# Differential attention: transposes ahead of the next item's scores, both maps in turns; output-scale copies and two weight loads first; GDN sums by direction

## What is computed

```python
def diff_attend(q, k, v, lam):          # 4 heads, 2 maps per head, 64 numbers each
    s = jnp.einsum('bqhcd,bnhcd->bhcqn', q, k, preferred_element_type=F32) * DIFF_QK ** -0.5
    pr = jax.nn.softmax(s, axis=-1)
    w = (pr[:, :, 0] - lam * pr[:, :, 1]).astype(v.dtype)
    return jnp.einsum('bhqn,bnhd->bqhd', w, v)

    def step(s, inp):                   # gated DeltaNet, per direction, chunk and head
        v_new = uc - jnp.einsum('bhck,bhkv->bhcv', wc, s)
        s_next = s * gl[..., None, None] + jnp.einsum('bhck,bhcv->bhkv', kt, v_new)
        o = jnp.einsum('bhck,bhkv->bhcv', qd, s) + jnp.einsum('bhcj,bhjv->bhcv', qkc, v_new)
        return s_next, o

    y = jnp.einsum(...)                 # merged branches @ w_out, times the layer's gate, plus residual
    new_lat = post_norm(h_lat, gate_x * out_x, ln_g[l], ln_b[l])
```

## Time and profile before

| | us |
|---|---|
| median of 3 runs | 2978.74 (2974.03 to 2988.12) |
| the profiled execution | 2976.96 |
| its span, first to last instruction | 2975.1 |
| PE busy | 2801.1 (94%) |
| DVE busy | 1541.9 (52%) |
| ACT busy | 1012.8 (34%) |
| mean granted TensorE clock | 0.987 |

### The profile page before, as it was taken

How to read it: one execution, slowest core, us unless ns; L and a number is a source line. 1 busy time by engine, 2 the same in 40 slices (tenths; PEclk the granted TensorE clock), 3 DMA queues, 4 the chain that set the end, 5 groups by cost and what they waited for, 6 DMA issues and landing times.

```text
span 2975.1 us, 44200 instructions
## 1 busy us (share of the span) xinstructions
PE 2801.1 (94%) x18238; PEld 2197.7 (74%) x18238; DVE 1541.9 (52%) x2683; ACT 1012.8 (34%) x1640; POOL 637.3 (21%) x261
## 2 busy tenths in 40 slices
PE   7999999999999999999997999899899999999997
PEld 1487888887788778886785438777776787887675
DVE  5546666326634443337745644667534554353756
ACT  0345343312222333224431234544332234332533
POOL 0121000222123111321023312100132331232036
PEclk9999999999999999999998999999999999999999
DMA  7511000324232112211134561000234321221034
GB/s 251 172 55 35 18 14 23 112 70 141 84 121 66 40 50 101 68 50 38 41 103 138 190 201 58 19 23 13 78 112 116 127 99 47 93 95 57 22 113 163
DMA packets 100453, 254.21 MB, mean 85 GB/s; under 512 B 10306, under 2 KB 32964, under 8 KB 99872
## 3 DMA queue, kind: packets, MB, share of 16 engines
q1 hardware_dynamic: 94314, 231.07, 23.8%
q10 hardware_dynamic: 5942, 20.33, 1.9%
HBM read 217.27 MB, written 34.08 MB: 84 GB/s over the span
## 4 chain that ended last, share of the span: by engine, by line
PE 77%; DVE 12%; ACT 4%; DMA 3%; issue 3%; POOL 1%; SPq 1%; ACTq 0%; DVEq 0%
PE ps L818 17%; PE ps L819 16%; PE ps L820 16%; PE ps L987 4%; PE ps L826 4%; PE ps L836 4%; PE ps L1315 3%; PE ps L1252 2%; PE ps L946 2%; PE ps L901 1%; DVE t_gcv L1956 1%; PE ps L930 1%; PE ps L1342 1%; DVE t_amx L2486 1%; DMA t_raw<-in_w_ada 1%
## 5 line engine op out<-in xcount | busy, mean ns | idle before, releaser
L779 POOL TENSOR_TENSOR t_wlo<-t_raw,t_whi 128x1024 fp32r<-128x1024 f32 x248 | 615.6, 2485 | 2306.7 <-ACT t_whi L1436 2306.6
L818 PE MATMUL ps<-t_u_hi,t_whi 128*128 128x512 f32 (+1 forms) x2368 | 862.7, 364 | 10.5 <-issue 4.2
L819 PE MATMUL ps<-t_u_lo,t_whi 128*128 128x512 f32 (+1 forms) x2368 | 831.7, 351 | 0.0
L820 PE MATMUL ps<-t_u_hi,t_wlo 128*128 128x512 f32 (+1 forms) x2368 | 828.8, 350 | 0.0
L1436 ACT ACTIVATE t_whi<-t_raw 128x1024 fp32r<-128x1024 f32 x248 | 262.3, 1057 | 936.0 <-PE ps L820 730.0
L818 PEld LDWEIGHTS ps<-t_u_hi,t_whi 128*128 128x128 f32 x2368 | 448.3, 189 | 85.9 <-issue 20.1
L819 PEld LDWEIGHTS ps<-t_u_lo,t_whi 128*128 128x128 f32 x2368 | 448.2, 189 | 62.1 <-issue 6.5
L820 PEld LDWEIGHTS ps<-t_u_hi,t_wlo 128*128 128x128 f32 x2368 | 446.3, 188 | 63.1
L836 PEld LDWEIGHTS ps<-t_grp 64*64 64x64 f32 x4608 | 155.9, 134 | 50.8 <-issue 28.2
L836 PE MATMUL ps<-t_grp 64*64 64x64 f32 x4608 | 177.4, 221 | 11.6 <-DVE t_grp L2285 5.3
L1507 ACT ACTIVATE t_grp<-ps 128x512 f32<-128x512 f32 (+2 forms) x236 | 107.2, 466 | 234.6 <-PE ps L836 181.4
(11 more groups left out here) (265 smaller groups left out, 3774.8 us busy)
## 6 DMA issues: line engine op xcount, KB each, us to landing
t_raw<-in_w_in SPq DMA_DIRECT2D x184, 512.0 KB, 3.7
t_raw<-in_w_ada SPq DMA_DIRECT2D x48, 512.0 KB, 4.2
t_raw<-in_w_br SPq DMA_DIRECT2D x32, 512.0 KB, 3.6
t_raw<-in_w_out SPq DMA_DIRECT2D x32, 512.0 KB, 3.7
t_sg<-gate_logits SPq DMA_DIRECT2D x28, 384.0 KB, 4.8
hs<-t_hstage ACTq DMA_DIRECT2D x20, 512.0 KB, 3.6
t_hring<-hs SPq DMA_DIRECT2D x20, 512.0 KB, 6.2
t_raw<-in_fwd SPq DMA_DIRECT2D x64, 128.0 KB, 3.0
```

Source lines behind the costliest of these rows:

```text
L779: pool.tensor_tensor(wlo[:, c % CONV, :], raw[:, s % RAW, :], whi[:, c % CONV, :].bitcast(f32), ALU.subtract).then_inc(sems["w_ready"], 1)
L818: pe.matmul(o, lh, rh, start=first, stop=False)
L819: pe.matmul(o, lh, rl, start=False, stop=False)
L820: return pe.matmul(o, ll, rh, start=False, stop=last)
```

## The change

Five edits. (1) SP loads two pieces of `w_out` right behind the fence and the other three behind the inputs of the next layer. (2) In `project_out` ACT's copies to `gb` come ahead of everything else. (3) The scores of an item are issued by stretches of keys with both maps in turns: both slots are claimed first. (4) For differential attention `scores(n + 1)` stands behind `turn_probs(n)`. (5) In the scan PE makes direction 0's q k ahead of direction 1's `within_chunk`; DVE adds the latter's result at level 2, with a wait on `g_oa` before direction 1's q k, and at the end of a round takes both sums of direction 0 before those of direction 1.

```diff
@@ -753,6 +753,7 @@
                 fenced(f0 + 10)
                 gate_loads(l, 3)
                 fenced(f0 + 11)
+                pieces(2)
                 if l + 1 < DEPTH:
                     layer_inputs(l + 1)
                     for dst, src in filter_inputs(l + 1):
@@ -760,7 +761,7 @@
                 load(lng[:, :, :], A["ln"][l], "ld_ln")
                 if l:
                     sp.wait_ge(sems["st_h"], 16 * NT)
-                pieces(5)
+                pieces(3)
                 for i in range(3):
                     skip_tile(l, i)
                 pieces(5)
@@ -1129,9 +1130,9 @@
                                            1 - d if lv == LEVELS - 1 else None), "g_pt")
                             lend("g_y", B + 1)
                         if lv == 1:
-                            if t and (l == 0 or chunk(t - 1, 1) < LT):
-                                within_chunk(1)
                             for d in range(2):
+                                if d and t and (l == 0 or chunk(t - 1, 1) < LT):
+                                    within_chunk(1)
                                 if outs[d]:
                                     B, tok = 3 * d, slice(cc[d] * P, (cc[d] + 1) * P)
                                     claim(B)
@@ -1306,16 +1307,18 @@
                 def scores(n):
                     h, q = its[n]
                     ka, kb = keys(q)
-                    for c in range(nh):
-                        i = (n * nh + c) % 2
-                        claim(2 * i, 2 * i + 1)
-                        r = slice(64 * c, 64 * c + 64) if diff else slice(0, P)
-                        for a in range(ka, kb, 512):
-                            b = min(a + 512, kb)
+                    for a in range(ka, kb, 512):
+                        b = min(a + 512, kb)
+                        for c in range(nh):
+                            i = (n * nh + c) % 2
+                            if a == ka:
+                                claim(2 * i, 2 * i + 1)
+                            r = slice(64 * c, 64 * c + 64) if diff else slice(0, P)
                             last = pe.matmul(slot(i)[:, a - ka:b - ka], aq[r, h, q * P:(q + 1) * P],
                                              ak[r, h if diff else h // 2, a:b], start=True, stop=True)
-                        ln.done(last, "at_s")
-                        lend("at_exp", 2 * i, 2 * i + 1)
+                            if b == kb:
+                                ln.done(last, "at_s")
+                                lend("at_exp", 2 * i, 2 * i + 1)
 
                 def turn_probs(n):
                     nk = (keys(its[n][1])[1] - keys(its[n][1])[0]) // P
@@ -1352,10 +1355,12 @@
                     scores(0)
                     yield
                     for n in range(len(its)):
-                        if n + 1 < len(its):
+                        if n + 1 < len(its) and not diff:
                             scores(n + 1)
                         yield
                         turn_probs(n)
+                        if n + 1 < len(its) and diff:
+                            scores(n + 1)
                         yield
                         if n:
                             weigh(n - 1)
@@ -1890,12 +1895,11 @@
 
             def project_out(l):
                 full = l == 0
+                for r in range(2 if full else 1):
+                    for n in range(2):
+                        ln.take("wo_gb")
+                        ln.done(run(gb[:, r, n * 512:(n + 1) * 512], ps[:, 6 + n, :], ACT.Copy), "wo_gb_ok")
                 for kind, a, b in projecting(l):
-                    if kind == "gb":
-                        for r in range(2 if full else 1):
-                            for n in range(2):
-                                ln.take("wo_gb")
-                                ln.done(run(gb[:, r, n * 512:(n + 1) * 512], ps[:, 6 + n, :], ACT.Copy), "wo_gb_ok")
                     if kind == "net":
                         sine(l + 1, a)
                     if kind == "out":
@@ -2284,10 +2288,12 @@
                                 continue
                             ln.step(dve.copy_predicated(y, over_heads(masks[:, 1 - d, lv, :]),
                                                         by_head(ps[:, B + 1, 0:256])), "g_y")
+                        if lv == 2 and t:
+                            within_chunk(t - 1, 1)
                         if lv == 1:
-                            if t:
-                                within_chunk(t - 1, 1)
                             for d in range(2):
+                                if d and t and (l == 0 or chunk(t - 1, 1) < LT):
+                                    dve.wait_ge(sems["g_oa"], ln.due["g_oa"] + 1)
                                 if outs[d]:
                                     B, c = 3 * d, cc[d]
                                     ln.take("g_qk")
@@ -2326,8 +2332,8 @@
                                                           ALU.mult, ALU.add)), "g_s")
                     for d in range(2):
                         between_chunks(t, d)
-                    for d in range(2 if t + 1 == NT else 1):
-                        within_chunk(t, d)
+                        if d == 0 or t + 1 == NT:
+                            within_chunk(t, d)
                 ln.skip(WOVEN)
 
             def out_norm(l, tok, ss, tmp):
```

## The result

| | before | after |
|---|---|---|
| median, us | 2978.3 (2974.03 to 2988.12, 4 runs) | 3056.76 (3054.26 to 3060.3, 4 runs) |
| the profiled execution, us | 2976.96 | 3054.26 |
| its span, us | 2975.1 | 3052.4 |
| mean granted TensorE clock | 0.987 | 0.975 |

The changed kernel takes 1.026 times as long, 95% interval 1.0232 to 1.0287. The forecast was 3054.

What follows compares the result with a forecast made beforehand. PE was busy 94% of the span, with DVE setting the pace in the attention item loop. From 2976.96, +64 +43 -20.5 -9 gave 3054 us, range about 3000 to 3090.

Steps and rivals of the forecast that it cites:

- Scores behind the transposes, +64: Differential attention loops: each item becomes one chain, wide ones 7.14 us instead of 4.90; layer 0 loses 36, layer 1 28.
- The clock, +43: Same loops: PE pauses 3.5 us in every wide item, lowering the clock; 1.4 us per item over 31 items.
- the clock that holds: Rival: PE's pauses in the attention loops cost no clock, giving 3011 us; chance 0.18.
- the clock that never comes back: Rival: all 31 items pay 2.2 us at half clock and gate units stretch too, giving 3089 us; chance 0.13.
- Both maps in turns, 0: Scores in the attention loops: behind the transposes nothing holds either map, so their order counts nothing; at best 10 us less.
- project_out, -20.5: Start of project_out: layer 0 gains 20, as PE goes on near 1579.5 instead of 1597.93; layer 1 gains 0.5.
- Sums by direction, -9: Scan: PE's wait for DVE's sum goes, 1.0 us per round over eight rounds, 0.5 in each last round; bounds -6 and -18.
- The faster rival: Attention loops: PE really sets the pace, DVE does not wait for scores, rows stay 4.9 apart; 2947 us; chance 0.05.
- Hidden in part: Rival: the loop's chain is shorter than 4.79 when DVE is not crowded, near 2985 us at best; chance 0.04.

Runs made afterwards that it cites:

- run with the pause filled: Changed kernel plus 12 useless float32 matmuls behind weigh in wide differential-attention items with no gate unit near; 3035.18 us, ratio 1.0186 to the kernel before.

## Why the prediction held, step by step

The sum was 64 + 43 - 20.5 - 9 = 77.5 on the profiled execution, and 77.3 came. That it fits so closely is luck: three terms were too large, two of them gains, and the opening's 4.4, which no edit makes, filled up what was missing. What was right is the mechanism, and the size of the largest term.

- **Scores behind the transposes, +64: right.** The run with the pause filled shows this term by itself. Layer 0: 149.2 - 113.0 = 36.2, predicted 36. Layer 1: 113.1 - 86.4 = 26.7, predicted 28. The item was put at 0.76 + 1.59 + 4.79 = 7.14 and is 7.24, the 0.10 being 0.05 until the transposes start and 0.05 more in them. A narrow item behind a narrow one was put at 3.90 and is 3.98. Of layer 1's three gate units only two stand between the two points that were compared, each 1.9 long beyond its item (predicted 2.1), so the sum had one too many there.
- **The clock, +43: right in kind, nearly a third too large.** Measured 15.4 + 17.4 = 32.8, that is 1.06 for each of the 31 items instead of 1.4. The price of an item at half clock was about right (predicted 2.2, measured 9.28 - 7.24 = 2.04). What was mis-sized is how many there are: the step was that the pause comes with every item. In layer 0 the short gate units fill it in one item of each head, the long ones bring the clock back in another, and only eight of the sixteen items pay, 1.4 to 2.0 each; the mean clock of 0.88 and 0.82 says that it was low for about a quarter and a third of the time. Both extreme rivals, the clock that holds and the clock that never comes back, are out.
- **Both maps in turns, 0: right**, in both orders of the loop.
- **project_out, -20.5: 17.0 came.** Counted back by 55.1, the delay until there, the network started at 1634.06 - 55.1 = 1579.0, where 1579.5 was said. Two steps failed. The 18.4 set this start of the network against 1597.93, the start of the product behind it; the network itself had started at 1596.06 before, so the forecast of 1579.5 was worth 16.6 and the measured start 17.1. And the 2 us for the clock did not come at all: from 1634.06 to 1640.70 it was 0.50, and the first matmul of the product takes 0.79 in both kernels. Also, the sum gave the gain to both edits together, and the runs show that either alone brings most of it.
- **Sums by direction, -9: the size failed**, 4.7 in this trace and about 3 over the kernels, both outside the bounds of 6 to 18. The step was "in the way next is DVE, 0.20 at 330.99", from which a gain of 1.0 per round was chosen. With PE earlier at that place the wait there grew from 0.2 to 1.0 on average (2.8 at most); of a wait of 10.9, 6.2 came back at it. The 0.20 of the trace was what was left of a wait that the wait before had been hiding.
- **The faster rival** fell at the place it named: DVE's rows in the loop stand 7.2 apart, not 4.9. **Hidden in part** fell as well, since the chain is 4.79 also when DVE has nothing else to do.

## What to carry to other kernels

Where two engines hand an item back and forth, the work that feeds the slower one has to be issued ahead of the work that waits for it: moving 1.6 us of scores behind a wait made a wide item 2.3 us longer, and the clock a further 1.1, while the matmuls themselves gained nothing. A wait that shows 0.2 us behind another wait is no bound for what comes after the first is cured; look at how much work the awaited engine has there. And two edits that cure the same wait are one gain, so run each alone before keeping both.

## What the runs showed of the hardware

- One map's 768 columns take 1.55 us alone and both maps' together 1.56, in turns or one after the other. The two halves of the rows work side by side without any help from the order in the program, and splitting the pair in two places of the program costs the whole of this. The Trainium skill (TensorEngine Tiling (Array Packing), "Key Properties") says that tiles work independently and in parallel; the trace agrees, 1.56 against 1.55.
- A loop with a pause of PE in nearly every item ran at half clock only part of the time: the low stretch shown above stands behind a pause of 4.88, an item behind a pause of 3.29 is at full clock, and in the run with the pause filled the clock fell behind one pause of 2.26 and held behind another of the same length. With work of no use in 8 items of layer 0's loop PE waited 25.0 us in all for finished weights instead of 45.0, and the clock stayed at 1.00. The filling cost nothing where it fitted into the pause.
- The first 338 us, the same program in every kernel, differed by up to 12 us between profiled executions.
